# Two dense down slots tile by tile, and the attention's value products moved behind them

## The reference, cut to what matters

```
x = x + mlstm_mixer(rmsnorm(x, g0))
x = x + swiglu_dense(rmsnorm(x, g1))          # width 2816
hk = rmsnorm(x, norm_kv);  h = rmsnorm(x, norm_mix[1])
kv = hk @ w_kv                                # six blocks of 256: compressed k and v, then k, v, k, v
q  = h @ w_q                                  # 16 heads of 64, and gates
x = x + nsa(q, gates, kv) @ w_out             # compressed, selected and window attention
x = x + moe_swiglu(rmsnorm(x, g2))            # the best two of eight experts
return rmsnorm(x, norm_final)
```

## Time and profile before

| | |
|---|---|
| median of 3 runs | 1375.59 us (1374.94 to 1375.81) |
| the profiled execution | 1374.47 us |
| its span, first to last instruction | 1372.6 us |
| busy share PE, DVE, ACT, POOL | 98%, 58%, 49%, 3% |
| mean granted clock of PE | 0.994 of 2.4 GHz |
| moved by DMA | 431.65 MB |

### The profile page before, as it was taken

One profiled execution on the slowest core, in us unless ns is written; L12 is line 12 of the kernel. 1 busy time (PEld: TensorE's weight loads), 2 busy tenths in 40 slices (PEclk: granted clock), 3 DMA queues, 4 the chain that ended last, 5 costly groups with the idle time before them and its releaser, 6 DMA issues.

```text
span 1372.6 us, 18637 instructions
## 1 busy us (share of the span) xinstructions
PE 1338.9 (98%) x7452; PEld 988.0 (72%) x7452; DVE 792.7 (58%) x880; ACT 673.5 (49%) x834; POOL 40.2 (3%) x96
## 2 busy tenths in 40 slices
PE   7999999998999998999999999999999999999997
PEld 7987888887986466786677666677666677666762
DVE  6855655545858858974267645257654357654332
ACT  5546544434657855763356534355534355543221
POOL 7000000001000000000000000000000000000000
PEclk9999999999999999999999999999999999999999
DMA  8543555554453025999999999999999999999996
GB/s 352 177 161 118 192 192 183 177 187 178 159 211 123 1 78 204 354 361 419 426 427 428 420 408 423 428 427 427 425 416 426 426 426 428 425 410 424 427 427 279
DMA packets 36085, 431.65 MB, mean 314 GB/s; under 512 B 4000, under 2 KB 4000, under 8 KB 5152
## 3 DMA queue, kind: packets, MB, share of 16 engines
q1 hardware_dynamic: 35856, 429.94, 77.7%
q10 hardware_dynamic: 144, 0.52, 0.1%
HBM read 429.40 MB, written 1.05 MB: 314 GB/s over the span
## 4 chain that ended last, share of the span: by engine, by line
PE 94%; DVE 2%; DMA 2%; ACT 1%; issue 0%; POOL 0%; POOLq 0%; SPq 0%; DVEq 0%; ACTq 0%
PE bank L1568 21%; PE bank L1570 20%; PE bank L1569 20%; PE bank L2071 13%; PE bank L2092 7%; PE bank L1916 2%; PE bank L1942 2%; DMA raw<-in_moe 1%; PE bank L2015 1%; PE bank L1926 1%; PE bank L2119 1%; PE bank L2130 1%; PE bank L1944 1%; DMA raw<-in_wts 1%; PE bank L2023 1%; DVE ht_lo L1014 1%
## 5 line engine op out<-in xcount | busy, mean ns | idle before, releaser
L1473 DVE TENSOR_TENSOR w_lo<-raw,w_hi 128x2048 fp32r<-128x2048 f32 x114 | 258.0, 2288 | 151.7 <-ACT w_hi L880 151.4
L1568 PE MATMUL bank<-w_hi,ht_hi 128*128 128x512 f32 (+1 forms) x768 | 302.3, 394 | 0.9 <-DVE ht_lo L1014 0.9
L1570 PE MATMUL bank<-w_hi,ht_lo 128*128 128x512 f32 (+1 forms) x768 | 296.4, 386 | 0.0
L880 ACT ACTIVATE w_hi<-raw 128x2048 fp32r<-128x2048 f32 x114 | 214.7, 1909 | 139.6 <-DMA raw<-in_moe 107.0
L982 DVE TENSOR_TENSOR w_lo<-raw,w_hi 128x2048 fp32r<-128x2048 f32 x73 | 166.6, 2289 | 109.7 <-ACT w_hi L556 109.5
L1569 PE MATMUL bank<-w_lo,ht_hi 128*128 128x512 f32 (+1 forms) x568 | 217.8, 384 | 0.0
L556 ACT ACTIVATE w_hi<-raw 128x2048 fp32r<-128x2048 f32 x74 | 141.4, 1918 | 95.1 <-PE bank L1570 92.8
L1568 PEld LDWEIGHTS bank<-w_hi,ht_hi 128*128 128x128 f32 x768 | 144.4, 188 | 44.2 <-issue 14.4
L1570 PEld LDWEIGHTS bank<-w_hi,ht_lo 128*128 128x128 f32 x768 | 144.3, 188 | 29.9
L1473 DVE TENSOR_TENSOR more_lo<-more,w_hi 128x2048 fp32r<-128x2048 f32 x50 | 114.3, 2290 | 81.4 <-ACT w_hi L880 81.3
L880 ACT ACTIVATE w_hi<-more 128x2048 fp32r<-128x2048 f32 x50 | 95.9, 1918 | 101.6 <-PE bank L1570 61.9
(11 more groups left out here) (334 smaller groups left out, 1587.3 us busy)
## 6 DMA issues: line engine op xcount, KB each, us to landing
raw<-in_moe SPq DMA_DIRECT2D x112, 2048.0 KB, 12.6
more<-in_moe SPq DMA_DIRECT2D x54, 2048.0 KB, 12.7
raw<-in_wts SPq DMA_DIRECT2D x71, 1024.0 KB, 4.8
more<-in_moe SPq DMA_DIRECT2D x4, 1024.0 KB, 15.0
xs<-in_x SPq DMA_DIRECT2D x2, 512.0 KB, 3.9
out<-xn SPq DMA_DIRECT2D x4, 256.0 KB, 2.1
pk<-in_packed SPq DMA_DIRECT2D x1, 517.0 KB, 7.8
g1b<-in_norm_ffn ACTq DMA_DIRECT2D x1, 512.0 KB, 3.6
```

Of the source, the lines that this page charges most:

```text
L880: a(w_hi[:, hi_order(n) % SPLIT, :], slot_raw(n), ACT.Copy).then_inc(s_hi, 1)
L1473: v.tensor_tensor(slot_lo(n), slot_raw(n), w_hi[:, hi_order(n) % SPLIT, :].bitcast(F32), ALU.subtract).then_inc(s_lo, 1)
L1568: mm(out_, sh, mh, start=first, stop=False)
L1570: return mm(out_, sl, mh, start=False, stop=last)
```

## The change

The last two down slots (51 and 52) are done by `down_two`, tile by tile, and tile 0 is turned within it, after 42 of its 48 matmuls. The two value slots become slots 53 and 54 (`VV0`), right behind; the keys, first queries, compression and last queries each move by two numbers. PE's order is then: `values(0, 0)`, the turn of tile 1, `values(1, 0)`, `values(0, 1)`, `values(1, 1)`, and the keys. High and low parts are made per tile and per pair of blocks (`stream_high`, `stream_low`), in the order that `TURNED` lists; tile 0 is turned into banks 4 to 7 and tile 1 into banks 2 and 3. The values stand in banks 0 and 1, one per tile, and are copied to SBUF behind the splits up to slot 56. The keys use banks 6 and 7, the compression's hidden layer 4 and 5. In the attention stage the value products and their copies are gone. The extra buffers in the key operands' area (`EXTRA_FREE`) are free after the fourth key slot. Work and results stay the same. Cut to its core (left out: the new semaphore, the changed bank numbers and counts that follow from it):

```diff
-    FF0, DN0, KV0, W10, VV0, BO0, N0 = 20, 42, 53, 59, 65, 67, 71
-    Q_SLOT = (57, 58, 63, 64)
+    FF0, DN0, VV0, KV0, W10, BO0, N0 = 20, 42, 53, 55, 61, 67, 71
+    Q_SLOT = (59, 60, 65, 66)
+    TURNED = ([(3, 0, b) for b in range(4)] + [(4, 0, 0), (4, 0, 1)] + [(3, 1, b) for b in range(4)]
+              + [(4, 0, 2), (4, 0, 3)] + [(4, 1, b) for b in range(4)])
...
-    EXTRA_FREE = (VV0 + 2, VV0 + 2, N0, N0 + 1)
+    EXTRA_FREE = (KV0 + 4, KV0 + 4, N0, N0 + 1)
...
+    def turned_at(t, k):
+        if t == 0:
+            return B[4 + k // 2][:, (k % 2) * P:(k % 2 + 1) * P]
+        return B[2 + k // 4][:, (k % 4) * P:(k % 4 + 1) * P]
+    def turned_count(p, t, b):
+        return 24 + TURNED.index((p, t, b)) + 1
+    def shared(t, b):
+        return b if t == 0 else b | 1
...
-        split_to(KV0 - 1 + AHEAD)
-        squares(2, 4)
-        ht_high(3, 3, 20, hk_hi)
-        ht_high(4, 4, 20)
+        split_to(VV0 + 1)
+        def stream_high(p, t, pairs):
+            for b in pairs:
+                if p == 3:
+                    act.wait_ge(s_xt, 20 + 4 * t + shared(t, b) + 1)
+                else:
+                    act.wait_ge(s_htl, turned_count(3, t, shared(t, b)))
+                for k in (2 * b, 2 * b + 1):
+                    ins = a((hk_hi if p == 3 else ht_hi)[:, k, t * P:(t + 1) * P], turned_at(t, k), ACT.Copy,
+                            scale=pk[:, C_GAIN + 8 * p + k:C_GAIN + 8 * p + k + 1])
+                ins.then_inc(s_hth, 1)
+        square(2, 0, 4)
+        stream_high(3, 0, range(4))
+        stream_high(4, 0, (0, 1))
+        square(2, 1, 4)
+        split_to(KV0)
+        stream_high(3, 1, range(4))
+        stream_high(4, 0, (2, 3))
+        stream_high(4, 1, range(4))
+        split_to(KV0 + 1)
+        for t in range(NT):
+            act.wait_ge(s_used, VV0 + 2)
+            a(vv[:, t, :, :], B[t][:, :].rearrange("p (b d) -> p b d", b=2), ACT.Copy).then_inc(s_vvc, 1)
...
-            split_to(Q_SLOT[i] + AHEAD)
+            split_to(min(Q_SLOT[i] + AHEAD, BO0 + 1))
...
-        def v_copied(i):
-            act.wait_ge(s_used, VV0 + i + 1)
-            a(vv[:, :, i, :], B[4 + i][:, :].rearrange("p (t d) -> p t d", t=2), ACT.Copy).then_inc(s_kva, 2)
...
-            if n in (2, 3):
-                v_copied(n - 2)
...
-        split_to(KV0 - 2 + AHEAD)
-        residual(1, (0, 1, 2, 3), KV0 - 1)
-        normed(2)
-        ht_low(3, 3, hk_hi, hk_lo)
-        ht_low(4, 4)
+        split_to(VV0 + 1)
+        def stream_low(p, t, pairs):
+            hi, lo = (hk_hi, hk_lo) if p == 3 else (ht_hi, ht_lo)
+            for b in pairs:
+                dve.wait_ge(s_hth, turned_count(p, t, shared(t, b)))
+                for k in (2 * b, 2 * b + 1):
+                    ins = v.scalar_tensor_tensor(lo[:, k, t * P:(t + 1) * P], turned_at(t, k),
+                                                 pk[:, C_GAIN + 8 * p + k:C_GAIN + 8 * p + k + 1],
+                                                 hi[:, k, t * P:(t + 1) * P].bitcast(F32), ALU.mult, ALU.subtract)
+                ins.then_inc(s_htl, 1)
+        residual(1, (0, 1, 2, 3), VV0 - 1, (0, 1))
+        normed_tile(2, 0)
+        stream_low(3, 0, (0, 1))
+        residual(1, (0, 1, 2, 3), VV0 - 1, (2, 3))
+        stream_low(3, 0, (2, 3))
+        normed_tile(2, 1)
+        stream_low(4, 0, (0, 1))
+        stream_low(3, 1, range(4))
+        split_to(KV0)
+        stream_low(4, 0, (2, 3))
+        stream_low(4, 1, range(4))
+        split_to(KV0 + 1)
...
-        def down_two(n, banks, kt0, first, last, turns, fresh=None):
+        def down_two(n, banks, kt0, first, last, turns, fresh=None, hi=hth, lo=htl):
...
-                            ins = mm3(B[banks[2 * t + half]][:, :], hth(kt, t), htl(kt, t),
+                            ins = mm3(B[banks[2 * t + half]][:, :], hi(kt, t), lo(kt, t),
...
-        for k in range(11):
-            pe.wait_ge(s_tpl, min(k + 1, 11))
-            down(DN0 + k, (0, 1, 2, 3), 2 * k, k == 0, k == 10, ath, atl)
-        transposed(3, 6)
+        for k in range(9):
+            pe.wait_ge(s_tpl, k + 1)
+            down(DN0 + k, (0, 1, 2, 3), 2 * k, k == 0, False, ath, atl)
+        pe.wait_ge(s_tpl, 11)
+        def stream_turned(t):
+            pe.wait_ge(s_xn, 5 + t)
+            for k in range(KD):
+                ins = nc.tensor.transpose(turned_at(t, k), xn[:, t, k * P:(k + 1) * P], ident[:])
+                if k % 2:
+                    ins.then_inc(s_xt, 1)
+        def values(i, t):
+            n = VV0 + i
+            wait_slot(n)
+            for k in range(KD):
+                if i == 0:
+                    pe.wait_ge(s_htl, turned_count(3, t, k // 2))
+                ins = mm3(B[t][:, i * 256:(i + 1) * 256], hk_hi[:, k, t * P:(t + 1) * P], hk_lo[:, k, t * P:(t + 1) * P],
+                          weights(w_hi, n, 256)[:, k, :], weights(w_lo, n, 256)[:, k, :], k == 0, k == KD - 1)
+            if t == NT - 1:
+                ins.then_inc(s_used, 1)
+        down_two(DN0 + 9, (0, 1, 2, 3), 18, False, True, {(1, 1, 0): lambda: stream_turned(0)}, None, ath, atl)
+        values(0, 0)
+        stream_turned(1)
+        values(1, 0)
+        values(0, 1)
+        values(1, 1)
+        pe.wait_ge(s_htl, turned_count(4, 0, 3))
         for i in range(4):
             if i >= 2:
                 pe.wait_ge(s_kva, 2 * (i - 1))
                 pe.wait_ge(s_kvd, 2 * (i - 1))
-            features(KV0 + i, B[4 + i % 2], None if i else 3, hk_hi, hk_lo)
-        pe.wait_ge(s_htl, 40)
+            features(KV0 + i, B[6 + i % 2], None, hk_hi, hk_lo)
+        pe.wait_ge(s_htl, turned_count(4, 1, 3))
+        pe.wait_ge(s_vvc, 2)
...
-        def values(i, t):
...
-        for t in range(NT):
-            values(0, t)
...
-            if n < 2:
-                values(1, n)
...
-    parts += [w_kv[:, :, b * 256:(b + 1) * 256] for b in (0, 1, 2, 4)]
+    parts += [w_kv[:, :, b * 256:(b + 1) * 256] for b in (3, 5, 0, 1, 2, 4)]
...
-    parts += [w_kv[:, :, b * 256:(b + 1) * 256] for b in (3, 5)]
```

More of the change, by code:

```diff
@@ L206, in trunk @@
     s_tp, s_tph, s_tpl = sem("act_transposed"), sem("at_hi_ready"), sem("at_lo_ready")
-    s_kva, s_kvd = sem("kv_copied_act"), sem("kv_copied_dve")
+    s_kva, s_kvd, s_vvc = sem("kv_copied_act"), sem("kv_copied_dve"), sem("values_copied")
     s_xf, s_xch = sem("blocks_ready"), sem("blocks_hi")
@@ L710, in _ @@
             act.wait_ge(s_used, KV0 + i + 1)
-            bank = B[4 + i % 2]
+            bank = B[6 + i % 2]
             lower = bank[0:64, :].rearrange("p (b t) -> p b t", b=2)
@@ L734, in _ @@
             act.wait_ge(s_used, W10 + 2 * c + 2)
-            a(hid[:, c, :], B[6 + c][0:G * NC_, 0:CH], ACT.Silu).then_inc(s_hid, 1)
+            a(hid[:, c, :], B[4 + c][0:G * NC_, 0:CH], ACT.Silu).then_inc(s_hid, 1)
         act.wait_ge(s_sf, 1)
@@ L820, in _ @@
         square(3, 0, 8)
-        tile_high(0, 6, 24, (0, 3, 6, 1))
-        tile_high(1, 6, 24, (4, 5, 2, 7), (0, 1))
+        tile_high(0, 6, 28, (0, 3, 6, 1))
+        tile_high(1, 6, 28, (4, 5, 2, 7), (0, 1))
         act.wait_ge(s_xu, 11)
@@ L826, in _ @@
         a(xn[:, 1, 512:D], xs[:, 1, 512:D], ACT.Square, accum_out=stats[:, 13:14]).then_inc(s_sq, 1)
-        tile_high(1, 6, 24, (4, 5, 2, 7), (2, 3))
+        tile_high(1, 6, 28, (4, 5, 2, 7), (2, 3))
         for t in range(NT):
@@ L1198, in _ @@
             dve.wait_ge(s_used, KV0 + i + 1)
-            upper = B[4 + i % 2][64:128, :].rearrange("p (b t) -> p b t", b=2)
+            upper = B[6 + i % 2][64:128, :].rearrange("p (b t) -> p b t", b=2)
             if i < 2:
@@ L1854, in _ @@
                     at = 960 * c + 60 * jj
-                    ins = mm3(B[6 + c][0:XM, 0:CH], xc_hi[:, at:at + XM], xc_lo[:, at:at + XM],
+                    ins = mm3(B[4 + c][0:XM, 0:CH], xc_hi[:, at:at + XM], xc_lo[:, at:at + XM],
                               weights(w_hi, n, CH)[:, j, :], weights(w_lo, n, CH)[:, j, :], jj == 0, jj == 15)
@@ L1935, in group_part @@
                 pe.wait_ge(s_ctc, 1 if t == FIRST_T else 2)
-                pe.wait_ge(s_kva, 12)
+                pe.wait_ge(s_kva, 8)
+                pe.wait_ge(s_vvc, 2)
                 if grp >= 2:
```

## The result

The changed kernel takes 1389.60 us (median of four runs, 1387.47 to 1390.70) against 1375.38 us before: a ratio of 1.0102, with an interval of 1.0088 to 1.0116. It is 1% slower, and the predicted 1377.2 us and its range up to 1380.0 us are wrong. In a second measurement, further down, the ratio was 1.0075.

The account below looks back on a forecast made before the run. The prediction took PE's chain of waits (94% through TensorE) as the bound. Handover +7.2, attention -6.5 and clock +0.9 gave +1.6 us on 1375.59, so 1377.2 us; range 1373.6 to 1380.0.

Parts of the forecast that it names:

- The handover: Down slots to first key slot's end: 11.09 us of value work enters, 3.9 is given back, +7.2 us.
- the pair's end: The two down slots done tile by tile, with tile 0's turn inside, were to end at 334.60.
- the remaining wait: PE's wait for tile 1's normed rows before the second tile's turn, predicted at 1.1 us.
- the fall of the earlier trace: Clock at 0.51 for 3.40 us behind the handover gap before the change, its 16 matmuls costing 1.55 us too much.
- The attention: First scores to first group product: S + 17.6 instead of S + 24.07, -6.5 us, with 4.6 us returning as waits.
- the first bias: VectorE's first score bias at the attention's start: 0.7 us behind S instead of S + 4.12.
- the rival without a fall: Clock does not fall in the attention: +0.7 us, 1376.3 us; chance 0.30.
- the late bias: Slot 68's split still precedes VectorE's first bias, moving all of attention by 3.4: +4.1, 1379.7 us; chance 0.14.
- the handover's wait: Tile 0's turn waits 1.45 us inside the down product: 1377.7 us without a clock fall, 1378.6 with; chance 0.10.
- the faster one: Attention without a hole, softmax keeping up with PE: -3.9 us, 1371.7 us; chance 0.08.
- The clock: A fall in the attention, priced between 0 and 1.55 us, 0.65 of it hidden by the copy's wait: +0.9 us.
- The hole at heads 2 and 3: S + 8.1 to S + 13.6, where PE was to lack work for 3.9 of 5.5 us, bringing a clock fall.

Follow-up runs that it names:

- second measurement: The changed kernel itself, unaltered, timed again on another chip beside the kernel before: 1385.37 us, ratio 1.0075.
- the run with the handover slot by slot: Changed kernel with four blocks of 24 dead matmuls in the attention, its last two dense down slots again done slot by slot: 1389.26 us, 1.0101.
- the waits filled: Changed kernel plus 18 dead dense matmuls ahead of the first scores and 12 each ahead of the third and fourth heads' transposes: 1375.02 us, 1.0003.
- score-shaped filler: Changed kernel with two, one and one dead matmuls of 64 rows by 512 columns in the same three attention waits: 1382.31 us, 1.0061.
- the run with two dead blocks: Changed kernel plus two blocks of 24 dead dense matmuls right behind the first compressed scores: 1388.37 us, 1.0097.
- the one with the wait ahead of S filled: Changed kernel plus 18 dead dense matmuls in the wait before the first scores, nothing added behind: 1385.88 us, 1.0067.
- one slot early: Half the change: only the first value slot moved early, the second left in the attention behind compressed scores and first transposes: 1378.05 us, 1.0046.
- four dead blocks: Changed kernel plus four blocks of 24 dead dense matmuls where the value parts stood before: 1382.33 us, 1.0063.
- score-shaped work: Changed kernel plus 3, 3, 2 and 2 dead matmuls of 64 rows by 512 columns where the value parts stood: 1381.90 us, 1.0059.

## Why the prediction was wrong, point by point

- **The handover was right.** The turn, the pair's end and the remaining wait are within 0.3 us. Predicted were +7.2 us up to the end of the first key slot. At the first scores it was +5.95 in the first measurement and +7.07 in the second, there counted from the first matmul of slot 51: 412.04 - 322.49 = 89.55 against 405.32 - 322.84 = 82.48. Most of what lies between the two is the pace of the key matmuls: by the three rows below, of before, of after and of the second measurement, three of them take (363.4 - 345.8)/50 = 0.352, (365.7 - 348.0)/52 = 0.340 and (370.2 - 347.9)/63 = 0.354 us, so 0.9 us between the last two for the 64 triples of four slots. These two are one kernel, so the change isn't the cause; what is stays open. The pair of slots is worth 2.5 us of the 4.0 that the handover gives back (11.09 - 7.07). The other 1.5 us are as much as the fall of the earlier trace rows had cost (1.55), and with the values there the clock no longer falls (granted 1.00 from 339.6 to 346.0 in the changed kernel, and in the run with the handover slot by slot).

```profile
L1568 PE MATMUL bank<-hk_hi,w_hi x51: 280/280/280, 345.8 to 363.4; 128*128 128x256 f32 x51
```

```profile
L1619 PE MATMUL bank<-hk_hi,w_hi x53: 276/276/277, 348.0 to 365.7; 128*128 128x256 f32 x53
```

```profile
L1619 PE MATMUL bank<-hk_hi,w_hi x64: 280/280/282, 347.9 to 370.2; 128*128 128x256 f32 x64
```

- **The attention was right, at full clock.** Predicted: the group product at S + 17.6, -6.5 us. With the waits filled it came at S + 18.12, and the turn behind it at S + 100.33 against 106.31 before: -5.98. The waits come in the order worked out; the first bias comes 1.3 us behind S instead of 0.7, about the half microsecond by which the group product is late. In that run S stands 412.34 - 322.62 = 89.72 us behind the first matmul of slot 51, which is +7.24. Sum: 7.24 - 5.98 = +1.3 us, within the interval of the measured 1.0003 (-1.0 to +1.8 us). It is the rival without a fall (+0.7 us). The rivals of the late bias and of the handover's wait did not occur, nor did the faster one.
- **The clock is the step that failed, in its size.** The prediction did take a fall, but bounded its price "above, the 1.55 us of the earlier trace rows", put it behind the wait at head 2 and counted +0.9 us of it; no rival had a longer one. That row shows a fall of 3.4 us with dense key matmuls right behind it (121 matmuls in 14.00 us). The attention without its values has no such block, and there the fall lasted 37.2 us. The measured price: turn at S + 112.79 against S + 100.33 with the waits filled, 12.5 us. In the second measurement it was 7.6: 519.92 - 412.04 = 107.88, against 512.46 - 412.15 = 100.31 in the profiled run with score-shaped filler on the same chip, whose clock held. In both profiled executions of the changed kernel the fall also came earlier than foretold, at the 2.13 us wait ahead of S, which was in the earlier trace rows all along and harmless there. The hole at heads 2 and 3, where it was foretold, starts falls as well, as the run with two dead blocks and the one with the wait ahead of S filled show.
- **What the Trainium skill was weighed for.** The Trainium skill's rule (TensorE: Matmul & The Clock Gate, Part 1, that activity alone releases the slow clock, and Part 4, that transposes don't count as such activity) did speak against this change, and the trace agrees with its direction: 37.2 us of scores, transposes and small products at 0.50. From 449.60 on, though, work of the same kind runs at 1.00 for 50.4 us, which the rule alone doesn't explain. The prediction counted +1.6 by that rule, with the price of a fall from another stage, where the work behind the fall was dense.

The cause is shown as far as this: the loss comes with the fall, and filling the waits removes it whole. That dense work ends a fall is likely: in two profiled executions a fallen clock came back nearly 3 us into a block of 24 dense matmuls. Against it stand three of ten runs of the kernel with one slot early, at a mean clock of 0.981 or 0.982 in spite of such blocks. What decides in a single execution whether the open wait starts a fall, and what ends it after 20, 27, 34 or 37 us without dense work, stays open.

## What to carry to other kernels

Before moving dense matmuls out of a stage of small ones, ask what would bring TensorE's clock back there, and price a fall by the work that stands behind it there (in this stage falls lasted 20 to 37 us without dense work), not by a fall of 3.4 us in a stage where dense work followed. A block of real dense work is worth most in a wait that the sparse stage has anyway: the same value products, half in the handover's gap and half in two of the attention's waits, beat both orders. To see what a change is worth apart from the clock, fill its waits with dead matmuls and time that.

## What was not expected of the hardware

- In the changed kernel the granted clock fell from 1.00 to 0.50 at a wait of 2.13 us, in front of the first scores; ahead of the wait PE had done 24 small matmuls in 1.5 us (407.67 to 409.14). The same wait behind the same matmuls passed without a fall in the profiled executions of the kernel before and of the runs with two and four dead blocks.
- PE busy without a pause left the clock down for long: 37.2 us of 37.2 busy at 0.50, with the attention's scores, transposes and products. Then it rose among work of the same kind; why it did so at that point isn't shown.
- Whether the shape of filler matters isn't shown. In the three waits, dense filler kept the mean clock at 0.995 or above in 12 of 12 runs, score-shaped filler in 1 of 5, but the latter left 3.88 us of the stretch without PE work against 1.66, and ran on another chip. In four blocks that left few gaps (20.86 - 20.09 = 0.77 us), score-shaped work held the clock in three of six runs.
